# Idle-filling matmuls on TensorE: identity times mask, ahead of two norms and the last modulations

## The reference

```python
mod = c_act @ ada_w[layer] + ada_b[layer]
sh1, sc1, g1, sh2, sc2, g2 = [m[:, None, :] for m in jnp.split(mod, 6, axis=-1)]
u = rms_norm(h, norm_mix_g[layer]) * (1.0 + sc1) + sh1
h = h + g1 * hybrid_mixer(u, w_in[layer], ..., w_out[layer])
u = rms_norm(h, norm_ffn_g[layer]) * (1.0 + sc2) + sh2
h = h + g2 * swiglu(u, ffn_w_gate[layer], ffn_w_up[layer], ffn_w_down[layer])
...
    y = mixed @ w_out[i]
    h = layer_norm(DEEPNORM_ALPHA * h + y, ln_g[i], ln_b[i])
```

## Time and profile before

| | us |
|---|---|
| median of 3 runs | 2173.61 (2172.82 to 2174.68) |
| the profiled execution, its own time | 2174.32 |
| its span in the trace, first to last instruction | 2172.5 |
| PE busy | 2070.2 (95%) |
| DVE busy | 1433.4 (66%) |
| ACT busy | 1065.4 (49%) |
| mean granted clock of TensorE | 0.985 |

### The profile page before, as it was taken

The page is one execution under the profiler, slowest core; times in us unless marked ns, Lnnn a source line. Parts: engine busy times, 40 slices in busy tenths (PEclk is TensorE's granted clock), DMA queues, the critical chain, the costliest instruction groups (busy, mean ns, idle before and its releaser), DMA issues.

```text
span 2172.5 us, 28328 instructions
## 1 busy us (share of the span) xinstructions
PE 2070.2 (95%) x9822; PEld 1701.3 (78%) x9822; DVE 1433.4 (66%) x2501; ACT 1065.4 (49%) x1963; POOL 88.8 (4%) x156
## 2 busy tenths in 40 slices
PE   6997999998979999999999999999999899999996
PEld 5776787887767887888888888787788688888885
DVE  6986788778878777655556556854465655555556
ACT  3543555555435444444544444454454555555542
POOL 2000011110002000000000000000000000000000
PEclk9997999999999999999999999999999999999998
DMA  9999778776767887666556665574466455555562
GB/s 320 369 370 282 246 258 258 241 253 205 269 241 250 274 255 258 194 194 189 187 191 194 190 191 184 177 240 129 149 193 215 138 163 172 171 164 174 173 220 92
DMA packets 281465, 468.86 MB, mean 216 GB/s; under 512 B 17120, under 2 KB 111552, under 8 KB 279936
## 3 DMA queue, kind: packets, MB, share of 16 engines
q1 hardware_dynamic: 278576, 451.32, 64.3%
q0 software_dynamic: 2768, 15.98, 2.2%
HBM read 465.13 MB, written 2.10 MB: 215 GB/s over the span
## 4 chain that ended last, share of the span: by engine, by line
PE 84%; DVE 7%; issue 5%; ACT 2%; DMA 1%; SPq 0%; POOL 0%; DVEq 0%; POOLq 0%; ACTq 0%
PE ps L536 25%; PE ps L538 25%; PE ps L537 24%; DVE w_lo L467 2%; PE ps L780 1%; DVE acc_a L446 1%; PE ps L752 1%; PE ps L1592 1%; PE ps L975 1%; PE ps L953 1%; PE ps L764 1%; ACT w_hi L420 1%; DMA X<-in_x 0%; DMA raw<-in_w_mem_kv 0%; DMA raw<-in_ada_w 0%
## 5 line engine op out<-in xcount | busy, mean ns | idle before, releaser
L467 DVE TENSOR_TENSOR w_lo<-raw,w_hi 128x512 fp32r<-128x512 f32 (+1 forms) x1328 | 904.5, 691 | 649.2 <-ACT w_hi L420 644.1
L420 ACT ACTIVATE w_hi<-raw 128x512 fp32r<-128x512 f32 (+1 forms) x1328 | 830.3, 629 | 1018.2 <-PE ps L538 978.3
L536 PE MATMUL ps<-w_hi,actT 128*128 128x512 f32 (+2 forms) x1920 | 776.8, 405 | 17.2 <-DVE w_lo L467 11.5
L538 PE MATMUL ps<-w_hi,actT 128*128 128x512 f32 (+2 forms) x1920 | 750.3, 391 | 0.0
L537 PE MATMUL ps<-w_lo,actT 128*128 128x512 f32 (+2 forms) x1920 | 749.2, 390 | 0.0
L536 PEld LDWEIGHTS ps<-w_hi,actT 128*128 128x128 f32 x1920 | 363.5, 189 | 101.3 <-DVE actT L650 11.5
L538 PEld LDWEIGHTS ps<-w_hi,actT 128*128 128x128 f32 x1920 | 363.1, 189 | 77.1
L537 PEld LDWEIGHTS ps<-w_lo,actT 128*128 128x128 f32 x1920 | 364.1, 190 | 70.2 <-issue 1.7
L536 PE MATMUL ps<-w_hi,hidT 128*128 128x512 f32 x352 | 138.3, 393 | 3.0 <-DVE w_lo L467 3.0
L538 PE MATMUL ps<-w_hi,hidT 128*128 128x512 f32 x352 | 137.1, 389 | 0.0
L537 PE MATMUL ps<-w_lo,hidT 128*128 128x512 f32 x352 | 137.0, 389 | 0.0
(11 more groups left out here) (286 smaller groups left out, 1564.8 us busy)
## 6 DMA issues: line engine op xcount, KB each, us to landing
raw<-in_w_in SPq DMA_DIRECT2D x208, 512.0 KB, 3.8
raw<-in_ada_w SPq DMA_DIRECT2D x192, 512.0 KB, 5.4
raw<-in_w_out SPq DMA_DIRECT2D x96, 512.0 KB, 4.2
raw<-in_ffn_w_gate SPq DMA_DIRECT2D x176, 256.0 KB, 2.9
raw<-in_ffn_w_up SPq DMA_DIRECT2D x176, 256.0 KB, 3.1
raw<-in_ffn_w_down SPq DMA_DIRECT2D x88, 512.0 KB, 3.7
raw<-in_w_kv_shared SPq DMA_DIRECT2D x48, 512.0 KB, 3.6
raw<-in_w_mem_kv SPq DMA_DIRECT2D x32, 512.0 KB, 7.4
```

The source lines that it names most:

```text
L420: act.activation(w_hi[:, g, 0:w], raw[:, slot_of(st, it), b, 0:w], ACT.Copy).then_inc(hi_ready, 1)
L467: nc.vector.tensor_tensor(w_lo[:, g, 0:w], raw[:, slot, b, 0:w], w_hi[:, g, 0:w].bitcast(f32), ALU.subtract).then_inc(blocks_read, 1)
L536: nc.tensor.matmul(o, hi, w_hi[:, g, 0:w], start=first_k, stop=False)
L538: last = nc.tensor.matmul(o, lo, w_hi[:, g, 0:w], start=False, stop=last_k)
```

## The change

A helper `keep_running(n, bank)` issues n matmuls of the identity (128x128, stationary) by the mask `cmask` (128x384, moving), both plain fp32, into a bank that nobody reads before it is written again. It is called with 18 matmuls into bank 4 between `wout` and the transposes of `u2`, and again between `out0` and those of `h1`. In `win_k`, `between_sums(taken, n)` first waits until `taken` sums were taken by DVE and then issues n of them into bank 6: 6 after the sum at ("A", 1, 0), 20 ahead of the sum in `start_c`, 4 behind it. PE also waits once for `dist`, ahead of `memkv`.

```diff
--- before.py
+++ after.py
@@ -1316,6 +1316,16 @@
 
             def u1_ready(g):
                 pe.wait_ge(turn_taken, TURNS["u1"] + g + 1)
+
+            def keep_running(n, bank):
+
+                for _ in range(n):
+                    nc.tensor.matmul(ps[:, bank, 0:384], ident[:, :], cmask[:, :], start=True, stop=True)
+
+            def between_sums(taken, n):
+                pe.wait_ge(ada_taken, 1 + taken)
+                keep_running(n, 6)
+            pe.wait_ge(S("dist"), 1)
             stage_matmuls(pe, "memkv", memT, as_columns=True, lead=lead, sum_at=2, carry=True, at={
                 ("w", 2, 3): lambda: turn_u1(0), ("w", 2, 5): lambda: turn_u1(1), ("w", 3, 0): lambda: turn_u1(2)})
             st_k = ST["win_k"]
@@ -1324,14 +1334,20 @@
                 ada_sum(pe, ST["memkv"], 0, 1, True)
                 u1_ready(0)
 
+            def sum_and_run():
+                ada_sum(pe, st_k, 0, 0, True)
+                between_sums(3, 6)
+
             def start_c():
+                between_sums(3, 20)
                 ada_sum(pe, st_k, 0, 1, True)
+                between_sums(4, 4)
                 u1_ready(6)
             stage_matmuls(pe, "win_k", actT, at={
                 ("w", 0, 0): start_k, ("w", 0, 1): lambda: u1_ready(1), ("w", 2, 1): lambda: turn_u1(3),
                 ("w", 0, 2): lambda: u1_ready(2),
                 ("w", 0, 3): lambda: u1_ready(3), ("w", 1, 3): lambda: turn_u1(4),
-                ("A", 1, 0): lambda: ada_sum(pe, st_k, 0, 0, True),
+                ("A", 1, 0): sum_and_run,
                 ("w", 0, 4): lambda: u1_ready(4), ("w", 1, 4): lambda: turn_u1(5), ("w", 0, 5): lambda: u1_ready(5),
                 ("A", 1, 8): lambda: turn_u1(6), ("w", 0, 6): start_c, ("w", 1, 6): lambda: turn_u1(7), ("w", 0, 7): lambda: u1_ready(7)})
 
@@ -1483,6 +1499,7 @@
             stage_matmuls(pe, "win", actT, width=WIN_W, sum_at=99, carry=True, each=beside_mixer)
             stage_matmuls(pe, "wout", actT, each=beside_mixer)
 
+            keep_running(18, 4)
             lead = turning(pe, "u2", lambda k, t: xn2[:, t, k * P:(k + 1) * P], quarter_ready("u2"))
             for i in range(3):
                 st = ST[f"gu{i}"]
```

## The result

| | before | after |
|---|---|---|
| median of 7 runs, us | 2174.11 (2171.32 to 2177.93) | 2182.05 (2179.45 to 2186.67) |
| the profiled execution, its own time | 2174.32 | 2183.4 |
| its span | 2172.5 | 2181.6 |
| mean granted clock of TensorE | 0.985 | 0.992 |

The ratio after / before is 1.0036, 95% interval 1.0026 to 1.0046: 7.8 us slower (5.7 to 10.0), where +4.5 was forecast. The time lies in the range and on the side that had the larger chance, but the sum of the terms is outside the interval, so at least one of them was wrong.

The account below looks back on a forecast made before the run. PE was taken as the bound, busy 95% of the span. Terms of -2.1 (`win_k`), +3.2 (`u2`) and +3.4 us (`h1`) gave +4.5, so 2173.61 + 4.5 = 2178.1 us; range 2174 to 2183.

Parts of the forecast that it names:

- The price of an added matmul: At all covers: 0.322 us a record, 0.645 us a call at full clock, taken from the pool mix.
- The rival of half the price: At all covers: an added matmul costs 0.32 us, so the kernel takes 2165.5 us; chance 0.08.
- the one of 1.2 GHz for all of them: At all covers: added matmuls run at 1.2 GHz, 23 us for 18, sum above +35 us; chance 0.02.
- `u2` and `h1`: At the two norms: eighteen matmuls outlast the wait, delaying the first product by 3.2 us at `u2`, 3.4 at `h1`.
- The early term: In `win_k`: the added 6, 20 and 4 matmuls together save 2.1 us.
- together -2.1 us at about 204 us: In `win_k`: sum of +0.3 and -2.4 us, the twenty having eaten the first place's 2.6 us lead.
- 12 x 0.23 + 0.36 = 3.1 us. Gain 2.9: At ("A", 1, 0): twelve products and a transpose group take 3.1 us at full clock instead of 5.96.
- 5.52 us from there: Behind the sum in `start_c`: time twelve products and a transpose group took in the kernel before.
- take 3.1 at the full clock: Behind the sum in `start_c`: the twelve products and transpose group shorten to 3.1 us, a gain of 2.4.
- 2 us or more: At `start_c`: how much the twenty matmuls' cover is too long, `acc_b` being complete at 191.45 or sooner.
- the clock gains don't come: Rival, in `win_k`: low clock returns or DVE and DMA can't follow; one missing about +7, both +9.8 us; chance 0.15.
- Taking back the delay: Rival, after the norms: up to 2.0 us of later DVE waits absorb the delay, giving 2176 us; chance 0.10.

Follow-up runs that it names:

- late18: Kernel before plus only the 18 matmuls ahead of `u2` and the 18 ahead of `h1`; 2180.48 us, ratio 1.0026.
- late12: Kernel before plus only 12 matmuls ahead of `u2` and 12 ahead of `h1`; 2173.06 us, ratio 0.9992.
- early: Kernel before plus only the 6, 20 and 4 matmuls in `win_k`; 2175.92 us, ratio 1.0009.
- early12: Kernel before plus only matmuls in `win_k`, 6, 12 and 4 in place of 6, 20 and 4; 2170.73 us, ratio 0.9983.
- after_again: The kernel after, unchanged, run once more for a second trace; one execution, 2181.19 us.
- all12: Kernel before plus 6, 12 and 4 matmuls in `win_k` and 12 each ahead of `u2` and `h1`; 2171.18 us, ratio 0.9983.

## Why the prediction was right or wrong

**The price of an added matmul** was right: 0.322 us a record (36 in 11.61 us at each norm, 40 in 194.31 - 181.41 = 12.90 us in `start_c`), 0.62 us a call by the times of late18 and late12. The rival of half the price falls with it, and so does the one of 1.2 GHz for all of them. The wait for `dist` cost nothing: the first product of `memkv` starts at 22.91 us before and at 22.90 after.

**`u2` and `h1`** were right: +3.27 and +3.55 us for +3.2 and +3.4, no idle time left in front of the transposes, and 0.47 us got back between them. Alone they measured +5.6 (3.3 to 7.8).

**The early term failed.** The step "together -2.1 us at about 204 us" was mis-sized: alone the early matmuls measured +2.0 us (0 to 3.9), and the three traces that have 6, 20 and 4 put them at about +0.1 (45.04 us to group 7 on the mean, against 44.90 for the four traces without early cover). Two parts of it are shown by the table. First, I took the low clock's price from a single trace, and it was the longest of the four: 46.15 us where the mean is 44.90, so 1.25 us of the gain was never there on average. The steps "12 x 0.23 + 0.36 = 3.1 us. Gain 2.9" and "5.52 us from there" treat rows of one execution as what always happens. Second, that the same piece would "take 3.1 at the full clock" behind the second sum supposed that the cover keeps the clock up. In two of the three traces it fell all the same, behind the one-column sum, and the four added matmuls outlasted the wait that was to hide them: +1.3 us in each. Together these are 1.25 + 0.83 (the mean of the three is that much above the first trace) = 2.1 of the 4.1 us between -2.1 and +2.0; another 0.2 is that the first trace itself gave -1.9 (44.21 for 46.15), not -2.1. The other 1.9 is inside the uncertainty of early's measurement, and its cause stays open. The trace of early has one thing that fits it, the fall behind the sum at 433 us, which costs 1.6 us and which the trace of before doesn't have; one trace doesn't say how often early's other executions have it.

That the time still lies in the stated range is owed to the width of the range and to the two norm terms, not to the term of `win_k`.

**The twenty were known to be too long**, by "2 us or more"; 4.7 it was in the trace. The -2.1 was therefore made of a gain at the first place and of nearly nothing at the second. early12 shows what the same idea brings when it fits: -3.7 us.

**The rival "the clock gains don't come"** was half true, which I had priced at "about +7" for one missing gain and given 0.15. The gain at ("A", 1, 0) came in eight of nine traces. The one at `start_c` came in the first trace and not in two others with the same twenty. Of its two reasons the first, that the low clock returns after the one-column matmuls, is what those two traces show. The second, that DVE or DMA can't follow, is not: with a DMA share of 1.02 PE had 28 records in 6 us at a clock of 1.00. So the mechanism that failed in the -2.1 had been named, and left out of the sum.

**Taking back the delay** did not happen beyond those 0.47 us.

**Not foreseen:** 4.6 us in the profiled execution of after that are not shown to come from the change. Its 49.19 us in the last column against 44.58 in the second trace of the same kernel are falls of the clock in the 64x30 products. One trace against one trace gave 9.1 us of span; the runs give 7.8, and the cause of the falls is not settled. That the change brings them is not borne out: early has no fall there and after_again one, as before has, and of the other kernels with early matmuls only all12 has more than one short fall, a single one about twice as long.

## What to carry to other kernels

A cover of unread matmuls is paid in full, 0.645 us a call here, for each one that outlasts the wait; cut it to end before the data come (12 for 18 and 20 turned +7.8 us into -3.7). It brings something only where dense products follow the wait directly at the low clock: at the two norms, where transposes and ACT's and DVE's work come first, even the well-cut cover gave 0.54 and 0.33 us. And a gain made of clock must be read from several traces, and to the end of the program: four executions of the same piece differed by 2.2 us, as much as the gain, and five traces that were quicker up to the first scores than before lost about 1.5 us or more again behind them.

The best versions measured, with 6, 12 and 4 in `win_k` and the 64x30 products in portions, are at 0.9982 and 0.9980 of the kernel before (without and with 12 at each norm), and beat both kernels.

## What the runs showed of the hardware

- Unbroken work ahead of a run of one-column matmuls does not by itself keep the clock up behind it. After sixteen one-column records the granted clock of the stretch 196 to 200 was 0.59 in one trace of the kernel after, so mostly 1.2 GHz, and 1.00, 2.4 GHz, in the other, with 13 us of unbroken 128x384 matmuls ahead of both. Of the seven traces that have four matmuls there, six show them slow (4.3 to 4.5 us for 2.85). Idle time is not needed for it: behind the sum at 433 us PE is busy without a gap, and the clock falls there in four of thirteen traces (0.72 in the stretch 435 to 441 of early, 1.00 in before).
- 64 records of 64x30 in a row let it fall in seven of ten traces, in the piece of program around them (44.6 us and more in the last column); 32 at a time, with large products between, in none of three.
- The same program loses the clock at different places in different executions. A mean granted clock says little about the time: after had 0.992 and was slower than before with 0.985.
